# Staggering where the low halves of two operand buffers begin

## What is computed

```python
def swiglu(u, w_in, w_out):
    a, b = jnp.split(u @ w_in, 2, axis=-1)
    return (jax.nn.silu(a) * b) @ w_out
```

## Time and profile before

| | |
|---|---|
| three runs | 2529.84, 2530.74, 2531.62 us; median 2530.74 |
| the profiled execution | 2532.03 us, of it 2530.2 us from the first to the last instruction |
| TensorE (PE) busy | 2445.1 us, 97% |
| TensorE weight loads (PEld) busy | 2226.9 us, 88% |
| VectorE (DVE) busy | 1801.1 us, 71% |
| ScalarE (ACT) busy | 1106.5 us, 44% |
| mean granted TensorE clock | 0.990 of full speed |

### The profile page before, as it was taken

How to read it: one execution, slowest core, us unless ns; L and a number is a source line. 1 busy time by engine, 2 the same in 40 slices (tenths; PEclk the granted TensorE clock), 3 DMA queues, 4 the chain that set the end, 5 groups by cost and what they waited for, 6 DMA issues and landing times.

```text
span 2530.2 us, 39280 instructions
## 1 busy us (share of the span) xinstructions
PE 2445.1 (97%) x15654; PEld 2226.9 (88%) x15654; DVE 1801.1 (71%) x3467; ACT 1106.5 (44%) x1656; POOL 0.2 (0%) x4
## 2 busy tenths in 40 slices
PE   4998999999999999999999999999999999998998
PEld 3998989999999888788888998888998888988997
DVE  7888887788977446768877669897785344676555
ACT  3444565544463324724223662232562222566443
POOL 0000000000000000000000000000000000000000
PEclk8999999999999999999999999999999999999999
DMA  8997656769855431653543256676374333122653
GB/s 317 334 332 266 211 193 191 250 234 313 304 196 188 140 100 59 208 159 125 154 141 121 85 183 202 192 237 199 119 241 148 94 125 95 62 92 91 202 185 99
DMA packets 161671, 454.72 MB, mean 180 GB/s; under 512 B 17745, under 2 KB 21329, under 8 KB 161489
## 3 DMA queue, kind: packets, MB, share of 16 engines
q1 hardware_dynamic: 161488, 452.21, 54.3%
HBM read 451.09 MB, written 1.05 MB: 179 GB/s over the span
## 4 chain that ended last, share of the span: by engine, by line
PE 77%; DVE 4%; ACT 4%; issue 1%; DMA 0%; ACTq 0%; DVEq 0%; SPq 0%
PE PS L1297 24%; PE PS L1299 24%; PE PS L1298 24%; DVE own L1803 1%; PE PS L1457 1%; PE PS L1324 1%; PE PS L1322 1%; ACT own L1525 1%; ACT Uh L1588 1%; PE PS L1506 1%; ACT NT L1592 1%; DVE X L1784 1%; PE PS L1489 0%; DVE X L1899 0%; ACT spare L1525 0%
## 5 line engine op out<-in xcount | busy, mean ns | idle before, releaser
L1297 PE MATMUL PS<-Uh,own 128*128 128x256 f32 (+1 forms) x2080 | 655.1, 315 | 30.4 <-DVE Ul L1888 21.7
L1298 PE MATMUL PS<-Ul,own 128*128 128x256 f32 (+1 forms) x2080 | 646.6, 311 | 0.0
L1299 PE MATMUL PS<-Uh,own 128*128 128x256 f32 (+1 forms) x2080 | 646.4, 311 | 0.0
L1525 ACT ACTIVATE own<-raw 128x1024 fp32r<-128x1024 f32 x425 | 443.3, 1054 | 360.9 <-PE PS L1299 298.6
L1803 DVE TENSOR_TENSOR own<-raw,own 128x1024 fp32r<-128x1024 f32 x425 | 515.0, 1220 | 76.6 <-ACT own L1525 76.2
L1297 PEld LDWEIGHTS PS<-Uh,own 128*128 128x128 f32 x2080 | 401.5, 193 | 55.4 <-issue 29.5
L1298 PEld LDWEIGHTS PS<-Ul,own 128*128 128x128 f32 x2080 | 401.8, 193 | 19.8 <-issue 0.2
L1299 PEld LDWEIGHTS PS<-Uh,own 128*128 128x128 f32 x2080 | 401.6, 193 | 19.7
L1297 PE MATMUL PS<-Hh,own 128*128 128x256 f32 (+1 forms) x1088 | 345.2, 317 | 0.0
L1298 PE MATMUL PS<-Hl,own 128*128 128x256 f32 (+1 forms) x1088 | 340.9, 313 | 0.0
L1299 PE MATMUL PS<-Hh,own 128*128 128x256 f32 (+1 forms) x1088 | 340.9, 313 | 0.0
(11 more groups left out here) (233 smaller groups left out, 3866.6 us busy)
## 6 DMA issues: line engine op xcount, KB each, us to landing
MODS<-in_mm SPq DMA_DIRECT2D x168, 256.0 KB, 3.8
SCR<-in_mm SPq DMA_DIRECT2D x136, 256.0 KB, 4.3
raw<-in_f0i SPq DMA_DIRECT2D x68, 512.0 KB, 4.2
raw<-in_f1i SPq DMA_DIRECT2D x56, 512.0 KB, 3.6
raw<-in_f2i SPq DMA_DIRECT2D x56, 512.0 KB, 3.6
SCR<-in_ma SPq DMA_DIRECT2D x88, 256.0 KB, 5.3
raw<-in_w1i SPq DMA_DIRECT2D x44, 512.0 KB, 5.4
raw<-in_w2i SPq DMA_DIRECT2D x44, 512.0 KB, 5.4
```

Source lines behind the costliest of these rows:

```text
L1297: e.matmul(o, ll, rh, start=start, stop=False, skip_group_check=shared)
L1298: e.matmul(o, lh, rl, start=False, stop=False, skip_group_check=shared)
L1299: return e.matmul(o, lh, rh, start=False, stop=stop, skip_group_check=shared)
L1525: e.activation(parts(w.n)[0], raw[:, w.n % RING, :], ACT.Copy).then_inc(s["whi"].tell(w.n), 1)
```

## The change

The low halves get other starts; nothing is added to or taken from the list of work, and no wait, shape or order changes. `Rows` is an indexing helper that turns `[p, k, cols]` into a slice of a flat tensor. Slot k of `Ul` begins 528 columns behind slot k - 1 (512 before), so it lies 64 k bytes later than it did against `Uh`. The slots of `Hl` lie 0, 16, 32, 48, 64, 96, 160 and 288 bytes later than they did against `Hh`. The memory for this comes from `CF` (60 keys' columns to 56) and from `T2`, which becomes columns 2048 to 2175 of `GW`: there the bias of group 0 lies, which the blocks c = 0, 1 and 2 read.

```diff
+class Rows:
+    def __init__(self, flat, starts):
+        self.flat, self.starts = flat, starts
+
+    def __getitem__(self, at):
+        p, k, cols = at
+        return self.flat[p, self.starts[k] + cols.start:self.starts[k] + cols.stop]
...
-        Ul = sb("Ul", [P, KT, 512], F32R)
+        Ul = Rows(sb("Ul", [P, KT * 512 + 16 * KT - 16], F32R), [528 * k for k in range(KT)])
         Hh = sb("Hh", [P, 2 * FS, 512], F32R)
-        Hl = sb("Hl", [P, 2 * FS, 512], F32R)
+        Hl = Rows(sb("Hl", [P, KT * 512 + 72], F32R),
+                  [512 * q + later for q, later in enumerate((0, 4, 8, 12, 16, 24, 40, 72))])
...
-        CF = sb("CF", [P, 60 * 8])
+        CF = sb("CF", [P, 56 * 8])
...
-        T2 = sb("T2", [P, P])
+        T2 = GW[:, 2048:2176]
...
-                    e.scalar_tensor_tensor(out=T2[:, :], in0=GW[:, 1024 + g * P:1024 + (g + 1) * P], scalar=vec("gb", c),
+                    e.scalar_tensor_tensor(out=T2, in0=GW[:, 1024 + g * P:1024 + (g + 1) * P], scalar=vec("gb", c),
...
-                        scalar=vec("gg", c), in1=T2[:, :].unsqueeze(1).broadcast_to([P, 4, P]), op0=ALU.mult,
+                        scalar=vec("gg", c), in1=T2.unsqueeze(1).broadcast_to([P, 4, P]), op0=ALU.mult,
```

## The result

Six runs of the changed kernel have a median of 2538.79 us (2537.20 to 2539.52), six of the kernel before 2532.18 us (2529.84 to 2534.75). The ratio is 1.0027 with a 95% interval of [1.0015, 1.0038]. The change makes the kernel slower by 6.6 us. The range of the prediction holds that time; its forecast, no change with a chance of 0.80, was wrong.

The account below looks back on a forecast made before the run. TensorE's matmul stream was taken as the bound; every part of the change was put at 0, leaving 2530.7 us, the median of the three runs before. Range 2526 to 2540 us, no change at 0.80.

Parts of the forecast that it names:

- What bounds the kernel: TensorE's matmul stream: busy 2445.1 of 2530.2 us, about 14,700 matmuls with 14 ns fixed each, some 205 us.
- I take 0, because the pitch is 120 ns ... at every distance of slot and weight block that comes up: TensorE reading low halves from new starts: 4277 matmuls, no change in time, as 120 and 226 ns steps repeat.
- The upper bound from plain float32: Plain float32 records of 256 columns start every 215 ns, hardly any fixed part, so no grid conflict makes the 14 ns.
- unless it strikes float32r alone: Exception for a grid conflict in float32r only: 4277 shifted low matmuls could lose 12 ns each, 51 us.
- The faster rival: Reading a low half 16 KiB behind its high half costs float32r a wait, now removed: 51 us less, 2480 us; chance 0.10.
- The slower rival: Unaligned starts cost TensorE an extra fetch on 1414 `Hl` matmuls: 2539 us at 6 ns, 2550 at 14; chance 0.10.
- Everything else at 0: VectorE's writes, moved scratch tensors and loads, spare weights and `T2` in `GW`: each put at 0 or within about 1 us.
- behind the matmul that runs: `spare` and `spare_gw` as weights, moved 736 bytes: loads of 190 and 193 ns stay hidden, so 0.
- The tests named in advance: Low matmuls by slot: faster, L1298 or L1299 at 107 to 109 ns; slower, 124 ns or more in `Hl` slots 1-3.
- The limit of 0.35 ns: Forecast wrong if the mean pitch of L1297 to L1299 moves by more than this: 5.1 us over 14,700 matmuls.
- The rule weighed against the row: 6 cycles beyond the columns means an estimated 109 ns, not 120; if placement caused the 11 ns, 4277 matmuls give 47 us.
- The other rule: TensorE's ports never wait on anyone, which would leave operand addresses no effect on matmul time.

Follow-up runs that it names:

- moved_only: Against the changed kernel: low halves no longer staggered, tensors kept as long, `T2` in memory of its own; 2532.44 us, ratio 1.0004 to the kernel before.
- the four scans: Against the kernel before: nothing staggered, pads move `Uh`/`Ul`, `Hh`/`Hl` and all from `SA` on by various distances; 2534.26, 2548.85, 2544.19, 2532.42 us.
- u_only: Against the kernel before: only `Ul` staggered, padded so that all behind it stays on the 512-byte grid; 2534.91 us, ratio 1.0015.
- t2_apart: Against the changed kernel: `T2` gets memory of its own again; 2538.38 us, ratio 1.0031 to the kernel before.
- place_by_width: Against the kernel before: `own` keeps weights for 512 columns on the grid, puts those for 256 columns 448 or 192 bytes off; 2511.33 us, ratio 0.9918.
- place_grid: Control for `place_by_width`: same memory, but every chunk of weights in the place a multiple of 256 bytes away; 2530.26 us, ratio 0.9995.

## Why the prediction was wrong

- **What bounds the kernel** was read rightly: TensorE's stream, with a fixed part beside the columns. Every change of time in this study came with a change of that stream's step.
- **"I take 0, because the pitch is 120 ns ... at every distance of slot and weight block that comes up"** is the step that failed. All distances that come up are multiples of 512 bytes, as the same paragraph says one sentence earlier, and 256 bytes is one turn: the trace compared distance 0 with distance 0. The rows could not speak for 64 or 16 bytes; they showed equality only where it had to be. A gap of evidence was taken for evidence.
- **The upper bound from plain float32** The earlier trace rows was read as a reason against, "on the same grid". Only their streams are on it. Added up from the tensor sizes, `ones`, their weights, begins 96 bytes off that grid modulo 256, so the rows didn't show these records at distance 0. Nor do they react as float32r does: in the kernel before, the changed one, `moved_only` and the four scans, where `X` on `ones` is at distances of 0, 64, 96, 128 and 160, its mean step stays between 215.2 and 217.2 ns. The records said nothing of float32r, and the prediction's own exception, "unless it strikes float32r alone", is what holds.
- **The faster rival** named the wrong pair. It asked about high half and low half; the pair that counts is weights and stream. A gain is real for 256 columns (up to 6.7 ns a matmul, against the 12 that it allowed). Its argument against, that the step from slot to slot equals the step from half to half, was true and told nothing, since both go over the same grid.
- **The slower rival** gave 2539 us, and 2538.8 was measured, but by another road. It put 6 ns on 1,414 `Hl` matmuls and nothing on U. In fact `u_only`, with 64-byte steps, already costs 0.15%, all three matmuls of a `three` are struck, 512 columns lose about 5 ns each, and 256 columns gain 2. A right sum of wrong terms.
- **Everything else at 0** held: L1915, L1927, L1835 and L2082 of the changed kernel keep their durations, the loads their landing times, and `t2_apart` clears `T2`. What lies behind the grown tensors was costed at 0 as well; `moved_only` confirms the sum and not the parts, since there 20 us won and 18 us lost cancel. Spare's place as weights, "behind the matmul that runs", was one of those parts.
- **The tests named in advance** were too narrow. Both looked for a rise or a fall in low matmuls, by slot. The limit of 0.35 ns for the mean step over all matmuls was not even reached: (9,738 x -1.90 + 4,632 x 4.96) / 14,370 = 0.31 ns. Kept apart by length, the step moved by 5 ns.
- **The rule weighed against the row.** The 6 cycles beyond the columns that the Trainium skill, "VectorE: DVE Perf Modes", gives in its section on the TRN2 errata were not reached by any float32r stream here. At 2.4 GHz a step of 120 ns is 288 cycles, 32 beyond the columns, and the shortest steady one, 113.3 ns, is 272, still 16 beyond. The other rule, from the Trainium skill, "SBUF — State Buffer", section on the two separate sides, is that TensorE's ports never wait on anyone. For VectorE and ScalarE the trace of the changed kernel agrees: 231.6 ns with 512 columns whether both are idle or both busy. But it doesn't leave "addresses nothing to do": `place_by_width` and `place_grid` differ in nothing but the place of the weights, and by 19 us.

## What to carry to other kernels

In this float32r stream, whose weights change at every matmul, the distance from weights to stream modulo 256 bytes changed the mean step of this kernel by up to 5.4 ns less on 120 (256 columns) and up to 7.4 ns more on 227 (512 columns). Read the step from the timeline for each length by itself, and set the two apart, by where the weights go. And before "the same wherever the trace can compare" is used as evidence, write down which values the trace compares.

## What the runs showed of the hardware that was not expected

The step of a float32r matmul depends on where weights and stream lie to each other, whichever of the two tensors is moved, with one turn at 256 bytes: with 512 columns 227 ns at distance 0, 229 at 64, 232.5 to 234 at the others tried; with 256 columns 120 at 0 and 96, 114.5 to 119 at the others. At distance 192 a stretch of 256 columns can run in either of two paces, about 113.3 or 117.7 ns. The step with 512 columns doesn't depend on VectorE or ScalarE: in the changed kernel the mean step with 512 columns is 231.6 ns where both are idle and 231.6 where both are busy. That it is TensorE's own weight loads and stream reads that meet in memory fits all of this, and was not shown: only their distance was varied, and no run took the loads away.
